# Tile 0's mixer in buffers of its own and the later mLSTM cells beside tile 0's experts, in a one-core hybrid block kernel

## Chip, cores and metric

The kernel runs on one core of a Trainium2 chip. The metric is the device time of one execution, in microseconds (us). Engines: PE (TensorE), DVE (VectorE), ACT (ScalarE), POOL (GpSimd) and SP (SyncE); the core has 16 DMA engines, fed by queues of SP, ACT and POOL.

## What is computed

One layer of a flow-matching backbone in float32, for 128 context tokens and 1024 latent tokens of width 1024:

```
h  = modulate(rmsnorm(x, n1), sh1, sc1)
mq, mk, mv, mo, gt, aq, ak, av = split_cols(h @ w_in)
m_out = mlstm_mixer(...)      # 4 heads of 128, forward and backward, h = h_f + h_b, rmsnorm, * sigmoid(mo)
a_out = attn_context(q, k, v, sink)                 # context tokens: one softmax over the 128 context keys + sink
a_out = attn_latent(rope(q), rope(k), v, kc, vc, sink)   # latent: 128 cached keys + neighbours within 128, + sink
x  = x + g1 * (concat(m_out, a_out) @ w_out)
h2 = modulate(rmsnorm(x, n2), sh2, sc2)
q  = (h2 @ w_q).reshape(N, 8, 256)                  # 8 heads, two halves of 128
sa, sb = q_a . sub_a, q_b . sub_b                   # 128 keys each; top 16 of each, then top 16 of the 256 sums
x  = x + g2 * sum over 8*16 experts of gate * gelu(h2 . u[e]) * v[e]      # rows u[e], v[e] of 1024 each
```

The context tokens use the conditioning row of c_ctx, the latent tokens that of c. The final mLSTM state of the context and its keys and values are outputs too. Each token picks its own 128 experts of 16384, so for one token 128 rows of u and 128 rows of v are fetched, 1 MB in all; for the 1152 tokens this is 1208 MB.

## The kernel before

**Stages.** The tokens are nine tiles of 128; tile 0 is the context, tiles 1 to 8 are latent. The stage `conditioning` computes the modulation rows, `project_in` (line 236) the input projection of all tiles, which it leaves in DRAM scratch (`qkT_scratch`, `kv_scratch`, `aqT_scratch`) at about 421 us. The stage `mix_and_experts` (line 654) does the rest and is the one that is changed.

**Generators.** Every engine runs the same five generators, each of which issues that engine's part of a step, and `drive` (line 715) calls them in one fixed order, so the order of every engine's queue is set in the source:

- `mixer(t)`: 15 sub-steps (SUBS). For each of 8 heads a score matmul over four key blocks of 128, mask and running minimum on DVE (L1560), exp on ACT, four transposes, four value matmuls; beside that the two mLSTM directions' h are loaded (L956 to L958), added and squared on POOL, normalised, multiplied by the sigmoid (L1095); then eight transposes, the w_out matmuls (L1241), and `at_x <- at_x, at_xn` (L1610), which is x1. Tile 0 goes through the same code with a mask of its own.
- `route(t)`: h2, the queries (16 chunks of w_q, 512 KB each), scores and the choice of experts. It has 34 steps (PART) for a first half of the heads' choice and 17 more for the second. The top-16 search begins with MAX8 (L1617) and ends, for each half of the experts, in `fx_eidx` (L1718) and `fx_gates` (L1729). For tiles 0 to 2 (STREAMED) w_q comes in chunks through two buffers `rt_wq` (four for the first eight chunks); from tile 3 on a resident copy is used, loaded from pair 30 (WQ_AT) of tile 2.
- `mlstm()`: 18 cells (here called units), forward and backward direction in turn, in three thirds each, and a finishing third of three steps; 57 thirds in all. A unit loads q, k, v (`ml_qkT`, `ml_k`, `ml_v`), and ends in `ml_h`, which ACT's queue stores (`h_scratch<-ml_h`). The first two units are tile 0; mixer 0 needs them alone, mixer t needs all units.
- `pair(t, r)`: 64 pairs per tile. A pair is two indirect gathers of 1 MB on POOL's queue (L1109, 128 rows of u and v each) into a ring of eight buffers, so that four pairs are under way; two dots on DVE (L1846), gelu (L1538) and the weights (L1542) on ACT, four accumulating matmuls on PE (L1396). The gather four pairs on is issued when PE has done the pair.
- `begin()`: what each engine waits for before the first gather.

**The order.** Six thirds of cells (LEAD), then the 15 sub-steps of mixer 0 with a third on each odd one; then the 34 first steps of route 0 with 43 thirds by `cells_beside`: one on each of the first six steps, 7 on the next eleven, 30 on the last seventeen. What is left of the cells comes next, then `begin`, whose POOL part waits for the h of all 18 units:

```
    pool.wait_ge(s_hd, UNITS)
    for d in range(2):
        pool.wait_ge(s_hst[d], 16 * TILES)
    for n in range(DEPTH):
        fetch(n)
```

After that the pairs run, and beside pair r of tile t `pace(t, r)` steps of the current tile's second choice and the next tile's route, and where `due(t, r)` says so one sub-step of the next mixer. In tile 0 mixer 1 stands beside pairs 0 to 14.

**Memory.** The mLSTM state buffers (`g.state`) and the mixer's (side "right", under an ExitStack `early`) take turns with others: the mixer has one set of buffers for all tiles, among it w_out (eight loads of 512 KB) and gate1, and w_q's resident copy overlaps it. The ring lies where the mLSTM state ends, so it can be filled only after the last cell. In PSUM the mixer's scores and tile 0's queries use `at_sP` (ST), the cells `fx_acc` and the two banks `rt_qP`.

## Time and profile before

| | us |
|---|---|
| median of 3 runs | 3687.01 |
| lowest and highest run | 3683.57, 3687.49 |
| the profiled execution, its own time | 3683.57 |
| its span | 3682.8 |
| stages before mix_and_experts, until about | 421 |
| first gather issued | 664.09 |
| first dot of experts | 673.56 |

The profile is one execution on the core. Its page gives the busy time of each engine: PE 72% of the span, DVE 67%, POOL 40%, ACT 27%. A second block shows the span in 40 slices of 92 us. A busy share of an engine says little here, since the program has two parts of different kind: until the first gather the engines work one after the other on small pieces with DMA used at 20 to 60%, afterwards the 1208 MB of expert rows pass.

### The profile page before, as it was taken

How to read it: one execution, taken by the hardware profiler on the slowest of the kernel's cores; microseconds unless marked ns; L12 is line 12 of the kernel's file. 1: busy time of each engine (PE TensorE's matmuls, PEld its weight loads, DVE VectorE, ACT ScalarE, POOL GpSimd, SP SyncE). 2: the span in 40 equal slices, each digit the busy share in tenths (PEclk: the TensorE clock that was granted, in tenths of full speed). 3: DMA queues.
4: the chain of work that ended last, by engine and by line, in shares of the span. 5: the costliest groups of instructions: out<-in, count | busy, mean ns of one | idle time of the engine just before them, and what ended most of it. 6: DMA issues, size and time to landing. Idle time of an engine off the chain costs nothing.

```text
span 3682.8 us, 31091 instructions
## 1 busy us (share of the span) xinstructions
PE 2644.4 (72%) x9770; PEld 1042.0 (28%) x9770; DVE 2453.7 (67%) x5523; ACT 990.0 (27%) x2700; POOL 1459.0 (40%) x1300
## 2 busy tenths in 40 slices
PE   7999888687877878866566567557656755775655
PEld 3455567333333333312121112112111211221111
DVE  3666435776787678648857677685767768576655
ACT  1223333442433244422122122212212221221111
POOL 0110023443454455434444444444444444444443
PEclk9999889899989989889799789879977987987677
DMA  7222446899999999999999999999999999999999
GB/s 299 95 97 94 163 125 204 333 410 422 416 421 426 425 412 420 389 424 414 427 427 427 427 423 427 422 417 424 416 427 420 427 420 423 424 417 427 411 427 380
DMA packets 224537, 1365.12 MB, mean 371 GB/s; under 512 B 25194, under 2 KB 36074, under 8 KB 75890
## 3 DMA queue, kind: packets, MB, share of 16 engines
q0 software_dynamic: 165888, 1208.03, 78.4%
q1 hardware_dynamic: 50992, 134.74, 10.1%
q10 hardware_dynamic: 7492, 20.36, 1.4%
q8 instruction: 77, 1.26, 0.1%
q14 instruction: 88, 0.72, 0.0%
HBM read 1334.05 MB, written 28.99 MB: 370 GB/s over the span
## 4 chain that ended last, share of the span: by engine, by line
DMA 40%; PE 20%; DVE 15%; issue 4%; POOL 4%; ACT 4%; SPq 0%; ACTq 0%; POOLq 0%; DVEq 0%
DMA fx_ring<-arg_uv,fx_eidx 38%; PE fx_acc L1396 11%; DVE fx_ring L1846 8%; POOL fx_ring L1109 4%; PE at_sP L1241 3%; ACT fx_weighted_pick L1542 2%; PE at_aP L1203 1%; DMA rt_wq<-arg_w_q 1%; DVE rt_rest L1708 1%; DVE rt_ab L1710 1%; DVE rt_rest L1706 1%; DMA rt_w_q<-arg_w_q 1%; PE at_sP L1269 1%; ACT fx_gelu L1538 1%; PE at_sP L1187 1%
## 5 line engine op out<-in xcount | busy, mean ns | idle before, releaser
L1396 PE MATMUL fx_acc<-fx_ring,fx_weighted_pick 128*64 128x512 f32 x4608 | 1417.7, 747 | 929.8 <-ACT fx_weighted_pick L1542 908.3
L1109 POOL DMA_INDIRECT fx_ring<-arg_uv,fx_eidx x1152 | 1317.0, 1143 | 1634.7 <-PE fx_acc L1396 1444.5
L1846 DVE CUSTOM_DVE_ANT_0 fx_ring<-fx_ring,fx_h 128x1024 f32<-128x1024 f32 x1152 | 1411.8, 1237 | 774.0 <-DMA fx_ring<-arg_uv,fx_eidx 769.5
L1396 PEld LDWEIGHTS fx_acc<-fx_ring,fx_weighted_pick 128*64 128x64 f32 x4608 | 327.0, 158 | 1903.7 <-ACT fx_weighted_pick L1542 1368.4
L1538 ACT ACTIVATE fx_gelu<-fx_dot 128x2 f32<-128x2 f32 x576 | 117.1, 203 | 2116.2 <-DVE fx_dot L1846 2115.7
L424 PE MATMUL in_z<-w_in,in_hT 128*128 128x512 f32 (+1 forms) x864 | 352.4, 566 | 7.3 <-PEq L97 7.3
L1542 ACT ACTIVATE fx_weighted_pick<-fx_weighted_pick,fx_gelu 128x64 f32<-128x64 f32 x1152 | 338.0, 340 | 55.1 <-ACT fx_gelu L1538 2.2
L424 PEld LDWEIGHTS in_z<-w_in,in_hT 128*128 128x128 f32 x864 | 163.6, 192 | 177.3 <-issue 172.0
L1269 PE MATMUL rt_qP<-rt_w_q,rt_h2T 128*128 128x512 f32 x384 | 193.6, 629 | 9.4 <-DMA rt_w_q<-arg_w_q 9.4
L384 POOL COPY in_turned<-in_heads 128x320 f32<-128x320 f32 x9 | 9.1, 1010 | 320.1 <-DVE in_heads L579 320.1
L1241 PE MATMUL at_sP<-at_w_out,at_mixT 128*128 128x512 f32 x288 | 133.3, 606 | 0.9 <-DVE at_mixT L1601 0.9
L1269 PEld LDWEIGHTS rt_qP<-rt_w_q,rt_h2T 128*128 128x128 f32 x384 | 66.8, 193 | 137.3 <-issue 126.3
L1838 DVE TENSOR_TENSOR fx_weighted_pick<-fx_pick,fx_gates 128x512 f32<-128x512 f32 x144 | 99.2, 689 | 2.4 <-DVE fx_gates L1729 0.7
L1846 DVE DVE_READ_ACCUMULATOR2_ANT fx_dot<- 128x1 f32 x1152 | 94.6, 82 | 0.0
L1560 DVE CUSTOM_DVE_ANT_0 at_s<-at_sP,at_mask,at_sink_negated 128x512 f32<-128x512 f32 x72 | 53.0, 750 | 60.7 <-PE at_sP L1187 50.9
L1538 ACT ACT_TABLE_LOAD x64 | 82.1, 1283 | 10.9 <-POOL ml_h L1129 9.7
L1269 PE MATMUL rt_qP<-rt_wq,rt_h2T 128*128 128x512 f32 x128 | 65.1, 632 | 15.1 <-DMA rt_wq<-arg_w_q 15.1
L1241 PEld LDWEIGHTS at_sP<-at_w_out,at_mixT 128*128 128x128 f32 x288 | 52.8, 191 | 78.1 <-issue 77.9
L1143 POOL TENSOR_TENSOR ml_k<-ml_k,ml_cols 128x512 f32<-128x512 f32 x18 | 18.7, 1039 | 141.2 <-ACT ml_cols L1506 108.9
L631 DVE SCALAR_TENSOR_TENSOR in_ada_acc<-in_ada_w,silu,in_ada_acc 128x1024 f32<-128x1024 f32 x56 | 70.1, 1292 | 0.3
L1203 PE MATMUL at_aP<-att_v,at_pT 128*128 128x64 f32 x432 | 67.8, 299 | 0.0
L1187 PE MATMUL at_sP<-att_kT,at_qT 64*128 64x384 f32 x144 | 65.4, 537 | 0.0
(300 smaller groups left out, 2450.4 us busy)
## 6 DMA issues: line engine op xcount, KB each, us to landing
rt_wq<-arg_w_q SPq DMA_DIRECT2D x44, 512.0 KB, 7.8
fx_ring<-arg_uv,fx_eidx POOLq DMA_INDIRECT x1152, 12.7
in_ada_w<-arg_w_ada SPq DMA_DIRECT2D x32, 512.0 KB, 4.0
ml_qkT<-qkT_scratch SPq DMA_DIRECT2D x18, 512.0 KB, 4.2
ada_w<-arg_w_ada SPq DMA_DIRECT2D x8, 1024.0 KB, 13.8
w_in<-arg_w_in SPq DMA_DIRECT2D x16, 512.0 KB, 16.4
rt_w_q<-arg_w_q SPq DMA_DIRECT2D x16, 512.0 KB, 32.7
kv_scratch<-in_kv ACTq DMA_DIRECT2D x9, 768.0 KB, 3.3
```

Source lines behind the costliest of these rows:

```text
L424: mm = pe.matmul(zp[b % 3][:, 0:n], hT[par][:, k, :], g.w_in[:, k, c0:c0 + n], start=(k == 0), stop=(k == KD - 1))
L631: dve.scalar_tensor_tensor(ada_acc[cnd][:], ada_w[m % AW][:], g.silu[:, k, cnd:cnd + 1], ada_b[:] if k == 0 else ada_acc[cnd][:], ALU.mult ...
L1109: pool.indirect_dma_start(out=ring[j][:], out_offset=None, in_=io.uv, in_offset=bass.IndirectOffsetOnAxis(ap=eidx[t % 2][:, i:i + 1], axis=0),
L1187: pe.matmul(ST[h % 2][:, P:4 * P], lhs, g.akT[half, t * P:t * P + 3 * P], start=True, stop=True).then_inc(s_sc, 1)
L1203: mm = pe.matmul(aP[:, h * ADH:(h + 1) * ADH], pT[h % 2][:, j * P:(j + 1) * P], rhs, start=(j == 0), stop=(j == 3))
L1241: mm = pe.matmul(ST[half][:], mixT[:, j, :], w_out[:, j, half * 512:(half + 1) * 512], start=(j == 0), stop=(j == KD - 1))
L1269: mm = pe.matmul(banks[half][b][:], hq2T[:, k, :], w[:, b * 512:(b + 1) * 512], start=(k == 0), stop=(k == KD - 1))
L1396: mm = pe.matmul(acc[b][cg * TOKS:(cg + 1) * TOKS, :], wsel[:, i % (2 * FILL), :], ring[i % GROUP][:, D + b * 512:D + (b + 1) * 512], star ...
L1538: act.activation(gelu[:, sl], dot[:, sl], ACT.Gelu_apprx_tanh).then_inc(s_gelu, 1)
L1542: last = act.activation(wsel[:, i, :], wsel[:, i, :], ACT.Copy, scale=gelu[:, i:i + 1])
L1838: dve.tensor_tensor(wsel[:, lo:lo + FILL, :], pick[:].unsqueeze(1).to_broadcast([P, FILL, TOKS]), gates[t % 2][:, r * NC:r * NC + FILL].un ...
L1846: dve.tensor_tensor_reduce(out=ring[j][:, 0:D], in0=ring[j][:, 0:D], in1=h2r[t % 2][cg][:], scale=1.0, scalar=0.0, op0=ALU.mult, op1=ALU.a ...
```

## The change

What it does, in five parts:

1. Tile 0's mixer has buffers of its own (`first`), all later tiles another set (`later`). w_out and gate1 are loaded for each set, and w_out is scaled by the norm weights for each. The ring lies where tile 0's mixer buffers end, no longer where the mLSTM state ends.
2. Tile 0's attention is `context(k)`: one key block, no mask, all heads in a few instructions.
3. The first eight chunks of w_q have six buffers (two `rt_wq`, the two rows of h2 of tile 0, one of tile 1, `gate2`), the next eight four.
4. The cells: 16 thirds stand beside mixer 0, 13 beside route 0, three after `begin`, the other 25 beside the first pairs of tile 0, one on each of 17 pairs and two after. `begin` waits for x1 of tile 0 (`at_x1_stored`), not for the cells.
5. In tile 0 mixer 1 stands beside pairs 23 to 37 and mixer 2 begins on even pairs after; route 1 begins at pair 38 (pair 17 before) with one or two steps per pair and ends at pair 63 (50 before). In tile 1 four pairs in five carry a sub-step; in tile 2 the resident w_q is loaded from pair 40 (30 before) and route 3 ends at pair 61 (57 before).

The core of the diff:

```diff
-    LEAD = 6
...
-    WQ_AT = 30
+    WQ_AT = 40
...
+    ROOM = 17640
+    CELL_PAIRS = 23
 
...
     def due(t, r):
+        if t == 0:
+            return r >= CELL_PAIRS and (r < CELL_PAIRS + SUBS or r % 2 == 0)
         if t == STREAMED - 1:
             return r < WQ_AT
-        return t == 0 and r < SUBS or 17 <= r < 23 or r >= 51 or r % 2
+        return r % 5 != 4
 
     def pace(t, r):
+        if t == 0:
+            return int(r < 17) if r < CELL_PAIRS + SUBS else 1 + int(r % 3 == 0)
         if t == STREAMED - 1:
-            return int(r < 17 or r >= WQ_AT - 1) + int(r >= 48 and r % 2)
+            return int(r < 17) if r < WQ_AT - 1 else 1 + r % 2
         return 1
 
-    def ahead(m):
-        return 2 * WQ if m < HQ else WQ
-
-    def cells_beside(k):
+    def buffer_of(m):
+        if m < HQ:
+            return m % 6
+        if m < NSIDE:
+            return (4, 5, 0, 1)[m % 4]
+        return m % WQ
+
+    def before(m):
+        return max((i for i in range(m) if buffer_of(i) == buffer_of(m)), default=None)
+
+    def loads(m):
+        return sum(buffer_of(i) == buffer_of(m) for i in range(m + 1))
+
+    def heads_before(t, context):
+        return context + (t - 1) * AH
+
+    def cells_in_mixer(k):
+        if k < 4:
+            return 3 if k == 0 else 2
+        return int(k < 10 or k == SUBS - 1)
+
+    def cells_in_route(k):
         if k < TURN:
             return 1
-        if k < TURN + 11:
-            return int(k % 3 > 0)
-        return 1 + int(k % 4 > 0)
+        return int(k % 4 == 0)
+
+    def cells_in_pair(r):
+        return 1 if r < 17 else 2
 
     def drive(begin, pair, mixer, route, mlstm):
 
         cells = mlstm()
-        for _ in range(LEAD):
-            next(cells)
         subs = chain.from_iterable(mixer(t) for t in range(TILES))
         for k in range(SUBS):
-            if k % 2:
+            for _ in range(cells_in_mixer(k)):
                 next(cells)
             next(subs)
         steps = chain.from_iterable(route(t) for t in range(TILES))
         for k in range(PART):
-            for _ in range(cells_beside(k)):
+            for _ in range(cells_in_route(k)):
                 next(cells, None)
             next(steps)
-        for _ in cells:
-            pass
         begin()
+        for _ in range(3):
+            next(cells)
         for t in range(TILES):
             left = steps_of(t) if t + 1 < TILES else steps_of(t) - PART
             for r in range(PAIRS):
                 for _ in range(min(pace(t, r), left)):
                     next(steps)
                     left -= 1
+                if t == 0 and r < CELL_PAIRS:
+                    for _ in range(cells_in_pair(r)):
+                        next(cells, None)
+                if t == 0 and r == CELL_PAIRS - 1:
+                    for _ in cells:
+                        pass
                 if due(t, r):
                     next(subs, None)
...
+        def mixer_buffers(n):
+            with ExitStack() as room:
+                def esb(name, shape, dt=F32):
+                    return room.enter_context(nc.sbuf_tensor(f"{name}_{n}", shape, dt))
+
+                m = Names()
+                m.w_out = esb("at_w_out", [P, KD, D])
+                m.aq = esb("at_qT", [P, AH // 2, P])
+                if n:
+                    m.mask = esb("at_mask", [P, 4 * P])
...
+        later = mixer_buffers(1)
+        with ExitStack() as room:
+            w_q = room.enter_context(nc.sbuf_tensor("rt_w_q", [P, KD, 2 * D], F32))
+        held = sb("mixer_room", [P, ROOM])
+        first = mixer_buffers(0)
         ring = [sb(f"fx_ring{i}", [P, 2 * D]) for i in range(GROUP)]
         gate2 = sb("fx_gate2", [P, D])
+        wq = [sb(f"rt_wq{i}", [P, HALF]) for i in range(WQ)]
         h2r = [[sb(f"fx_h2_0_{i}", [P, D]) for i in range(NC)], h2r1]
+        wq += h2r[0] + [h2r1[1], gate2]
...
-        w_q = sb("rt_w_q", [P, KD, 2 * D], side="right")
...
-        eP = acc[0][:].rearrange("p (h n) -> p h n", n=P)
-        oE = acc[0][:].rearrange("p (h n) -> p h n", n=256)
-        R = [x[:].rearrange("p (h n) -> p h n", n=256) for x in (acc[1], qP[0], qP[1])]
+        eP = other[0][:].rearrange("p (h n) -> p h n", n=P)
+        oE = other[0][:].rearrange("p (h n) -> p h n", n=256)
+        R = [x[:].rearrange("p (h n) -> p h n", n=256) for x in (other[1], qP[0], qP[1])]
         misc = cP[:].rearrange("p h n -> p (h n)")
-        qP0, cP0 = ST, aP[:].rearrange("p (h n) -> p h n", n=P)
+        first.ST, later.ST = acc, other
+        qP0, cP0 = acc, aP[:].rearrange("p (h n) -> p h n", n=P)
...
+                def load_weights(cnd):
+                    m = later if cnd else first
+                    sp.dma_start(m.gate1[:], g.gate_dram[cnd:cnd + 1, :].to_broadcast([P, D])).then_inc(s_g1, 16)
+                    for k in range(KD):
+                        sp.dma_start(m.w_out[:, k, :], io.w_out[k * P:(k + 1) * P, :]).then_inc(s_wo, 16)
...
+                        if k == 0 and t == 1:
+                            load_head(1)
+                            load_weights(1)
...
                 def begin():
-                    for d in range(2):
-                        sp.wait_ge(s_hst[d], 16 * TILES)
+                    sp.wait_ge(s_x1o, 16)
+                    sp.wait_ge(s_qd, NSIDE)
                     sp.dma_start(gate2[:], g.gate_dram[COND:COND + 1, :].to_broadcast([P, D])).then_inc(s_g2, 16)
...
                 def begin():
-                    pool.wait_ge(s_hd, UNITS)
-                    for d in range(2):
-                        pool.wait_ge(s_hst[d], 16 * TILES)
+                    pool.wait_ge(s_x1o, 16)
                     for n in range(DEPTH):
                         fetch(n)
...
                 def begin():
-                    pe.wait_ge(s_hd, UNITS)
+                    pe.wait_ge(s_qT, NG)
+                    pe.wait_ge(s_h2d, NC)
...
                 def begin():
-                    for d in range(2):
-                        dve.wait_ge(s_hst[d], 16 * TILES)
+                    pass
...
+                    def context(k):
+                        for b in range(2):
+                            for j in range(AH // 2):
+                                h = b * (AH // 2) + j
+                                half = slice(b * ADH, (b + 1) * ADH)
+                                cols_j = slice(j * P, (j + 1) * P)
+                                if k == 0:
+                                    mm = pe.matmul(m.ST[b][:, cols_j], m.aq[half, j, :], g.akT[half, P:2 * P],
+                                                   start=True, stop=True)
+                                    if j == AH // 2 - 1:
+                                        mm.then_inc(s_sc, 1)
+                                if k == 2:
+                                    if j == 0:
+                                        pe.wait_ge(s_p, (b + 1) * (AH // 2))
+                                    mm = pe.transpose(m.ST[b][:, cols_j], m.s[b][:, cols_j], g.ident[:])
+                                    if j == AH // 2 - 1:
+                                        mm.then_inc(s_pTp, 1)
+                                if k == 4:
+                                    if h == 0:
+                                        pe.wait_ge(s_pT, 2)
+                                    mm = pe.matmul(aP[:, h * ADH:(h + 1) * ADH], m.pT[b][:, cols_j],
+                                                   g.av[:, 1, b * ADH:(b + 1) * ADH], start=True, stop=True)
+                                    if h == AH - 1:
+                                        mm.then_inc(s_pv, 1)
+
...
+                        if t == 0 and k == 1:
+                            for h in range(AH):
+                                cols_h = slice(h % 4 * P, (h % 4 + 1) * P)
+                                if h == 0:
+                                    act.wait_ge(s_nm, 1)
+                                act.activation(m.s[h // 4][:, cols_h], m.ST[h // 4][:, cols_h], ACT.Exp, bias=m.nmx[:, h:h + 1],
+                                               scale=float(ADH) ** -0.5, accum_out=m.rs[:, h:h + 1]).then_inc(s_p, 1)
+                            act.wait_ge(s_dif, 1)
+                            act.activation(m.es[:], m.es[:], ACT.Exp).then_inc(s_es, 1)
...
+                        if t == 0 and k == 1:
+                            for b in range(2):
+                                dve.wait_ge(s_sc, b + 1)
+                                ca.link(dve.tensor_reduce(m.mx[:, 4 * b:4 * b + 4], m.ST[b][:].rearrange("p (h n) -> p h n", n=P),
+                                                          AX.X, ALU.max))
+                            ca.link(dve.tensor_scalar(m.mx[:], m.mx[:], -float(ADH) ** -0.5, None, ALU.mult))
+                            dve.tensor_tensor(m.nmx[:], m.mx[:], nsink[:], ALU.min).then_inc(s_nm, 1)
+                            dve.wait_ge(s_nm, 1)
+                            dve.tensor_tensor(m.es[:], sink[:], m.nmx[:], ALU.add).then_inc(s_dif, 1)
```

**What stands in the queues.** DVE at the end of tile 0's first choice of experts. Before (names with ml_ are cells, `fx_eidx` and `fx_gates` are what the gathers and their weights need, L1846 is the first dot):

```order
L1706 TENSOR_TENSOR rt_rest<-rt_pos_partf,rt_iota 128x1024
L1708 TENSOR_TENSOR rt_rest<-rt_rest,rt_val 128x1024 [waits rt_dve_chain]
L1710 TENSOR_REDUCE rt_ab<-rt_rest 128x64 [waits rt_dve_chain]
L1770 SCALAR_TENSOR_TENSOR ml_c<-ml_c,ml_tile_decay,rt_qP 128x129 [waits ml_c_done,ml_cols_ready,rt_dve_chain]
L1770 SCALAR_TENSOR_TENSOR ml_c<-ml_c,ml_tile_decay,rt_qP 128x129
L1775 TENSOR_TENSOR ml_num<-ml_num,fx_acc 128x258 [waits ml_intra_done,ml_inter_scaled]
...
L1718 SCALAR_TENSOR_TENSOR fx_eidx<-rt_ab 64x32 x4
...
L1729 TENSOR_TENSOR fx_gates<-rt_gexp,rt_gsum 64x32 x3
L1838 TENSOR_TENSOR fx_weighted_pick<-fx_pick,fx_gates 128x512 [waits fx_h2_rows_act,ml_h_stored1,fx_h2_rows_dve,ml_h_stored0,rt_route_done]
L1846 ISA fx_ring,fx_dot<-fx_ring,fx_h_0_0 128x1024 [waits fx_fetched0]
```

and now:

```order
L1813 TENSOR_REDUCE rt_ab<-rt_rest 128x64 [waits rt_dve_chain]
L1821 SCALAR_TENSOR_TENSOR fx_eidx<-rt_ab 64x32 [waits rt_dve_chain]
...
L1832 TENSOR_TENSOR fx_gates<-rt_gexp,rt_gsum 64x32 x3
L1857 TENSOR_TENSOR ml_e<-at_sP,ml_e 128x512 [waits ml_e_masked,ml_qk_done,rt_route_done]
L1873 SCALAR_TENSOR_TENSOR ml_c<-ml_c,ml_tile_decay,rt_qP 128x129 [waits ml_c_done,ml_cols_ready]
...
L1940 TENSOR_TENSOR fx_weighted_pick<-fx_pick,fx_gates 128x512 [waits fx_h2_rows_dve,fx_h2_rows_act]
L1948 ISA fx_ring,fx_dot<-fx_ring,fx_h_0_0 128x1024 [waits fx_fetched0]
```

The cell rows have left the way to `fx_gates`, the waits for stored h are gone, and one unit stands between the gates and the first dot.

POOL around the first gather, before:

```order
L1129 TENSOR_TENSOR ml_h<-ml_num,ml_den 128x512 [waits ml_den_ready,ml_h_stored0]
L1129 TENSOR_TENSOR ml_h<-ml_num,ml_den 128x512 [waits ml_den_ready,ml_h_stored1]
L1109 DMA fx_ring<-arg_uv,fx_eidx 128x2048 [waits ml_h_stored1,rt_route_done,ml_h_stored0,ml_h_ready]
L1109 DMA fx_ring<-arg_uv,fx_eidx 128x2048 x7
L1109 DMA fx_ring<-arg_uv,fx_eidx 128x2048 [waits fx_pair_done]
```

and now:

```order
L1162 DMA fx_ring<-arg_uv,fx_eidx 128x2048 [waits rt_route_done,at_x1_stored]
L1162 DMA fx_ring<-arg_uv,fx_eidx 128x2048 x7
L1196 TENSOR_TENSOR ml_k<-ml_k,ml_cols 128x512 [waits ml_load0,ml_cols_ready]
L1202 AFFINE_SELECT ml_e<-ml_e 128x512 [waits ml_e_ready]
L1175 COPY ml_rfix<-gate_rows 128x128 [waits ml_colT_done]
L1182 TENSOR_TENSOR ml_h<-ml_num,ml_den 128x512 [waits ml_den_ready,ml_h_stored1]
L1162 DMA fx_ring<-arg_uv,fx_eidx 128x2048 [waits fx_pair_done]
```

The first eight gathers wait for tile 0's choice and x1, and POOL's work of a unit stands among the later gathers.

DVE where tile 1's first gates are made, before (between the dots of pairs 50 and 51 of tile 0):

```order
L1846 ISA fx_ring,fx_dot<-fx_ring,fx_h_0_1 128x1024 [waits fx_fetched5]
L1846 ISA fx_dot 128x1
L1718 SCALAR_TENSOR_TENSOR fx_eidx<-rt_ab 64x32 x4
L1722 TENSOR_REDUCE rt_gsum<-rt_gexp 128x4 [waits rt_gate_exp,rt_dve_chain]
...
L1846 ISA fx_ring,fx_dot<-fx_ring,fx_h_0_0 128x1024 [waits fx_fetched6,rt_route_done]
```

and now:

```order
L1948 ISA fx_ring,fx_dot<-fx_ring,fx_h_0_1 128x1024 [waits fx_fetched7]
L1948 ISA fx_dot 128x1
L1821 SCALAR_TENSOR_TENSOR fx_eidx<-rt_ab 64x32 x4
...
L1832 TENSOR_TENSOR fx_gates<-rt_gexp,rt_gsum 64x32 x3
L1940 TENSOR_TENSOR fx_weighted_pick<-fx_pick,fx_gates 128x512 [waits fx_h2_rows_dve,fx_pair_done,fx_h2_rows_act,rt_route_done]
L1948 ISA fx_ring,fx_dot<-fx_ring,fx_h_1_0 128x1024 [waits fx_fetched0]
```

`fx_eidx` of tile 1 now stands behind the last dot of tile 0 (pair 63), and the gather of pair 0 of tile 1 waits for it (`rt_route_done`).

## Rows read from the trace of the kernel before

**Rows 1.** The page: span, DMA share in 40 slices (tenths), GB/s.
```profile
span 3682.8 us, 31091 instructions
...
DMA  7222446899999999999999999999999999999999
GB/s 299 95 97 94 163 125 204 333 410 422 416 421 426 425 412 420 389 424 414 427 427 427 427 423 427 422 417 424 416 427 420 427 420 423 424 417 427 411 427 380
```

**Rows 2.** The chain that ended last, by engine.
```profile
DMA 40%; PE 20%; DVE 15%; issue 4%; POOL 4%; ACT 4%; SPq 0%; ACTq 0%; POOLq 0%; DVEq 0%
```

**Rows 3.** The DMA view of 665 to 3683 us; last column us to landing.
```profile
DMA packets 183683, 1265.25 MB, mean 419 GB/s; under 512 B 20400, under 2 KB 20400, under 8 KB 36094
...
rt_wq<-arg_w_q SPq DMA_DIRECT2D x30, 512.0 KB, 8.1
```

**Rows 4.** SP's timeline: time, duration, line, out<-in.
```profile
472.32 0.33 SPq L956 DMA_DIRECT2D at_mix<-h_scratch  x1
```

**Rows 5.** DVE's timeline: start us, duration us; in brackets idle before and its releaser.
```profile
519.90 0.69 DVE L1610 TENSOR_TENSOR at_x<-at_x,at_xn 128x512 f32<-128x512 f32 x1
...
577.63 0.65 DVE L1617 MAX8 rt_val<-rt_scores 128x8 f32<-128x128 f32 x3
...
581.51 0.69 DVE L1754 TENSOR_TENSOR ml_e<-fx_acc,ml_e 128x512 f32<-128x512 f32 x1 [3.04 <-PE fx_acc L1366]
...
653.09 0.69 DVE L1754 TENSOR_TENSOR ml_e<-fx_acc,ml_e 128x512 f32<-128x512 f32 x1
...
659.78 1.52 DVE L1718 SCALAR_TENSOR_TENSOR fx_eidx<-rt_ab 64x32 uint32<-64x32 f32 x4
...
661.80 0.79 DVE L1729 TENSOR_TENSOR fx_gates<-rt_gexp,rt_gsum 64x32 f32<-64x32 f32 x4
...
673.56 1.23 DVE L1846 CUSTOM_DVE_ANT_0 fx_ring<-fx_ring,fx_h 128x1024 f32<-128x1024 f32 x1 [9.60 <-DMA fx_ring<-arg_uv,fx_eidx]
```

**Rows 6.** A window: us, busy PE, PEld, DVE, ACT, POOL; PEclk, DMA share, GB/s.
```profile
577.60:662.60 85.00, 68.64 (x480) 55.34 (x479) 60.23 (x211) 27.95 (x99) 26.99 (x35) 0.97 0.54 178
```

**Rows 7.** DVE's groups in 577.6 to 662.6 us.
```profile
L1770 DVE SCALAR_TENSOR_TENSOR ml_c<-ml_c,ml_tile_decay,rt_qP 128x129 f32<-128x129 f32 x36 | 10.9, 344 | 4.7 <-PE rt_qP L1375 4.5
...
L1775 DVE TENSOR_TENSOR ml_num<-ml_num,fx_acc 128x258 f32<-128x258 f32 x18 | 7.5, 417 | 0.0
...
L1754 DVE TENSOR_TENSOR ml_e<-fx_acc,ml_e 128x512 f32<-128x512 f32 x9 | 6.2, 689 | 18.6 <-PE fx_acc L1366 14.6 <-issue 3.9
...
L1779 DVE SCALAR_TENSOR_TENSOR ml_den<-ml_num 128x4 f32<-128x4 f32 x9 | 3.8, 422 | 0.3
```

**Rows 8.** POOL's timeline: the first gather.
```profile
664.09 1.14 POOL L1109 DMA_INDIRECT fx_ring<-arg_uv,fx_eidx  x1 [3.05 <-DMA h_scratch<-ml_h]
```

**Rows 9.** DMA issues of the whole span: count, KB each, us to landing.
```profile
ml_qkT<-qkT_scratch SPq DMA_DIRECT2D x18, 512.0 KB, 4.2
...
ml_k<-kv_scratch SPq DMA_DIRECT2D x18, 256.0 KB, 4.8
...
h_scratch<-ml_h ACTq DMA_DIRECT2D x18, 256.0 KB, 2.0
...
at_w_out<-arg_w_out SPq DMA_DIRECT2D x8, 512.0 KB, 9.5
...
at_qT<-aqT_scratch SPq DMA_DIRECT2D x9, 256.0 KB, 7.7
...
at_gate<-gate_scratch SPq DMA_DIRECT2D x2, 512.0 KB, 6.8
```

**Rows 10.** The page's groups: the dots beside the gathers, ACT's table loads.
```profile
L1846 DVE CUSTOM_DVE_ANT_0 fx_ring<-fx_ring,fx_h 128x1024 f32<-128x1024 f32 x1152 | 1411.8, 1237 | 774.0 <-DMA fx_ring<-arg_uv,fx_eidx 769.5
...
L1538 ACT ACT_TABLE_LOAD x64 | 82.1, 1283 | 10.9 <-POOL ml_h L1129 9.7
```

**Rows 11.** POOL, line 1095, in 421 to 664 us.
```profile
L1095 POOL TENSOR_TENSOR at_mix<-at_mix,at_sigmoid 128x512 f32<-128x512 f32 x1 | 1.3, 1274 | 0.1
```

**Rows 12.** POOL, line 1095, in 800 to 1500 us.
```profile
L1095 POOL TENSOR_TENSOR at_mix<-at_mix,at_sigmoid 128x512 f32<-128x512 f32 x6 | 12.8, 2140 | 0.5
```

367 lines of the change are left out of this document (188 added, 179 removed).

## The prediction

> **What bounds the kernel now.** I read the page first, for the two halves of the span. Until slice 8 the DMA engines are busy two to six tenths of the time; from there to the end every slice says 9, and where nothing disturbs them they move 427 GB/s [rows 1]. The DMA view of the stretch after the first gather gives 1265.25 MB in 3018 us, 419 GB/s on average [rows 3]. That half is bound by bytes: an engine's work there costs nothing unless it keeps the queue of gathers from being refilled, and every MB put there costs 1/427 GB/s = 2.34 us. The chain of waits agrees: DMA holds 40% of the span in it [rows 2]; the PE, DVE and ACT steps on it lie mostly between a landed gather and the issue of the one four pairs later, and so beside the others' transfers.
>
> The half before is bound by short dependent steps. In the last 85 us before tile 0's gates PE is busy 68.6, DVE 60.2, DMA 0.54 of the time [rows 6]: no engine is full, and the order decides. So the time is the moment of the first gather plus the bytes behind it, plus what bubbles there are. I take these terms in turn. The profiled execution's own time (3683.57) is 0.8 over its span and 3.4 under the median 3687.01.
>
> **Term 1, the first gather comes earlier.** It is issued at 664.09 [rows 8]. Three stretches lead there. (a) Until x1 of tile 0, at 520.6 [rows 5]. h of tile 0 is asked for at 472.32 [rows 4]; it waits for units 0 and 1 being stored, and that stays. Behind it stand eight heads over four key blocks with mask, now eight matmuls over one block, and 7 cell thirds instead of which 16 now lie partly before and partly inside the wait for h. I take 12 us off; the bounds are 0 (the h chain alone decides) and 20. (b) From x1 to the first MAX8 at 577.63, 57 us [rows 5]. 13 thirds stood beside these steps, now 9. One third costs 2.98 us: ml_e is at 581.51 and after eight more units at 653.09, 8.95 us a unit [rows 5]. Four thirds are 12; I take 10. (c) From there to the gates at 661.80, 85 us, in which nine units' worth of DVE work stands [rows 7]: 30 thirds by 2.98 are 89, so the cells set this stretch. Now four thirds stand there. DVE's own work for the choice is 60.2 less 10.9, 7.5, 6.2 and 3.8, about 32 [rows 6, 7], 36 with the small den rows not shown; with the four thirds and PE's scores I take 40, so 45 us go. (d) The gather waited 3.05 us for the last stored h, 1.5 of them behind the gates [rows 8]; that goes. Sum: 12 + 10 + 45 + 1.5 = 68, bounds 50 and 80. The first gather should be at about **596**.
>
> **Term 2, bytes moved behind the first gather.** From [rows 9]: w_out a second time 8 x 0.524 = 4.19 MB, gate1 0.52; tile 1's at_qT and mask, which stood in the first half, 0.52; the cells whose loads come after the gate, seven by 0.524 + 0.262 + 0.262 = 7.34 MB; ten h stores by 0.262 = 2.62. Together 15.2 MB, by 2.34 us **+36**. The second half has no free DMA time that could hide it.
>
> **Term 3, cells beside the first 21 pairs.** A pair's rows take 2.10 MB / 427 = 4.9 us; with the cells' bytes (one third per pair, 1.3 MB per three) some 6.0. Beside that DVE has two dots of 1.24 [rows 10], reads, fill, up to 2.1 of route steps and a third's 0.9, in all 5.4 to 5.7. ACT has to change its table between gelu and the cells' exp, 1.283 us each time [rows 10], perhaps twice a unit. All lie just under 6.0, so DMA should stay first; for the pairs where a third delays PE's four matmuls, and with them the next gather by more than the four pairs' slack, I put **+5**, bounds 0 and 31 (below).
>
> **Term 4, route 1 in pairs 38 to 63.** 34 steps in 26 pairs instead of one per pair, with w_q's chunks through two buffers that take 8.1 us to land [rows 3]. Two steps then need two chunks in a pair of 5 us every third pair; the mean need is 16 chunks in 22 pairs, 110 us, against 8.1 x 8 = 65 with two under way. **+2**, bounds 0 and 10.
>
> **Term 5, the boundary of tiles 0 and 1.** `fx_eidx` of tile 1 now stands behind the dots of pair 63. The gathers of tile 1 can only be asked for after it, so nothing is in flight when the last pair of tile 0 has landed. The dots are 1.2 more, from the start of the eidx rows to the end of the gates 2.8 (659.78 to 662.59 [rows 5]), and from the first issue to the first dot the trace shows 673.56 - 664.09 = 9.5 [rows 5, 8], of which 2.5 is the transfer itself: 1.2 + 2.8 + 7.0 = **+11**. Below, 5: some of the gates' work is done before the last row lands; above, 20, if route 1's last chunks are late too. The Trainium skill, page "DMA: Bandwidth & Descriptors", section "🔬 Anatomy of one DMA — SWDGE (gpsimd) path", gives a fixed cost of about 2.0 us per such DMA beside its bytes; by that the bubble would be some 6, an estimate from the page, and the sum 5 lower. The trace here, with 9.5 us for a first gather, speaks for more.
>
> **Term 6.** Route 3 ends at pair 61 of tile 2 instead of 57, still ahead of the last: **+1**, bounds 0 and 5. Later load of the resident w_q and the other places of mixer 1 and 2 cost nothing while DMA is full: the bytes are the same. The six buffers for w_q's chunks take waits away where PE is what is waited for; they are inside term 1(b). The second scaling of w_out is four DVE rows in tile 0, under the transfers.
>
> Sum: -68 + 36 + 5 + 2 + 11 + 1 = -13: 3683.6 - 13 = 3670.6 for the execution; on the median **3674**. 0.2%, about what a measurement of this kernel can tell from no change, is 7.4 us: the borders are 3679.6 and 3694.4.
>
> **The rivals.**
> *A, nothing comes back* (0.15). The gates stand in time, the cells hide: -68 + 36, about 3655. For it: DVE and ACT are each under a pair's time. Against: the order puts the eidx behind the last dot.
> *B, the cells set the pace of the first pairs* (0.16). ACT's part of a third waits for PE, which stands behind the same pair's matmuls, and ACT's gelu of the next pair stands behind that. If in two of three thirds this is served one after the other, 19 thirds by 2.98 are 57, less the 28 that their bytes already cost in term 2: +29, 3703, slower. It decides when pair and third together last longer than 6.1 us. For it: a third took 2.98 us even with no pair beside it, with DVE busy only 0.71 of that time [rows 6]. Against: four pairs lie in the ring.
> *C, mixer 0 ends no sooner* (0.09): h is asked for at the same time and the 16 thirds fill what the attention leaves. -68 becomes -56: 3686.
> *D, POOL slows DVE or is slowed* (0.10). POOL's multiply of mix and sigmoid took 1.27 us with DVE alone beside it [rows 11] and 2.14 beside the gathers and dots [rows 12], 0.87 more. Ten units have two such operations each: up to 17 us if they hold the next gather, 3691. By the Trainium skill, page "SBUF — State Buffer", section "🔬 SBUF: two separate sides", a DVE instruction with two SBUF inputs and a GpSimd one that reads SBUF share a port pair as an exclusive lock, and whichever starts first blocks the other for its whole length; the dots have two SBUF inputs, so by this rule each POOL row of a cell can wait a dot, or a dot a row. The two rows agree with it.
>
> **How the numbers follow.** The forecast has 0.50; its own range is 3658 to 3686, 0.38 of it faster, 0.12 within. A is faster (0.15). B is slower (0.16). C is 0.06 within, 0.03 slower. D is half within, half slower (0.05 each). So faster 0.53, same 0.23, slower 0.24. The range takes the low end of the forecast with half of A, 3648, and the high end of B's middle, 3706.
>
> **What would show it.** In the profile after: the first gather at about 596 (term 1), with x1 near 508, MAX8 near 555 and the gates near 595; about 1280 MB behind it (term 2); pairs of 6.0 to 6.2 us in the first 21 of tile 0 with DMA at 0.97 or more (term 3; B shows 7 or more with DMA at 0.8); a hole of about 11 us in DMA's use at the end of tile 0, with the first gather of tile 1 released by DVE (term 5). The prediction is wrong if the first gather is after 615, if the DMA share in the first pairs falls under 0.9, or if other such holes stand at later tiles.

## The result, and the profile after

The change takes 3729.61 us (median of 5 runs, 3723.91 to 3748.80) against 3687.01 (3683.57 to 3688.84): a ratio of 1.0124, 95% interval 1.0102 to 1.0147. It is slower by some 43 us; 3674 were forecast, 3648 to 3706 as the range. The profiled execution (span 3747.1) is the longest of the five, some 19 us above the median, so its losses below are somewhat larger than the usual ones.

The page of the change, the lines that answer to [rows 1] and [rows 2]:

```profile
span 3747.1 us, 30887 instructions
...
DMA  7222548999889999999999999999999999999998
GB/s 293 97 98 86 189 138 336 353 356 387 328 360 393 425 376 397 377 415 402 408 427 427 426 420 427 420 427 422 419 420 420 427 417 425 421 418 427 418 427 367
...
DMA 38%; PE 22%; DVE 15%; issue 5%; POOL 5%; ACT 4%; SPq 0%; ACTq 0%; POOLq 0%; DVEq 0%
```

The transfers begin sooner (336 GB/s in slice 7, 204 before), but slices 9 to 20, most of tiles 0 to 2, move 328 to 425 GB/s where they moved 389 to 427. From slice 21 on the two pages read alike.

The marks of tile 0 on DVE's and POOL's timelines of the change, which answer to [rows 5] and [rows 8] (start, duration):

```profile
502.46 1.29 DVE L1713 TENSOR_TENSOR at_x<-at_x,at_xn 128x512 f32<-128x512 f32 x1
...
548.20 0.68 DVE L1720 MAX8 rt_val<-rt_scores 128x8 f32<-128x128 f32 x3 [9.38 <-ACT rt_scores L1567]
...
587.55 0.79 DVE L1832 TENSOR_TENSOR fx_gates<-rt_gexp,rt_gsum 64x32 f32<-64x32 f32 x4
```

```profile
589.26 1.15 POOL L1162 DMA_INDIRECT fx_ring<-arg_uv,fx_eidx  x1 [11.52 <-DVE fx_gates L1832]
```

The first gather is issued at 589.26, 74.8 us sooner than before. The DMA view from 589 to 3747 us answers to [rows 3]:

```profile
DMA packets 192186, 1279.93 MB, mean 405 GB/s; under 512 B 21040, under 2 KB 24624, under 8 KB 44592
```

14.7 MB more lie behind the first gather, 34 us at 427 GB/s. To see where the rest went I cut both traces at the first gather of certain pairs: tile 0 at pairs 17, 26, 38 and 48, and tiles 1 and 2 whole. The columns are the stretch, its us, busy PE, PEld, DVE, ACT and POOL, granted clock, DMA share and GB/s. The change:

```profile
589.26:688.80 99.54, 66.67 (x331) 36.34 (x332) 77.13 (x220) 35.26 (x102) 51.07 (x55) 0.83 1.00 406
688.80:763.70 74.90, 48.54 (x202) 23.50 (x202) 46.48 (x95) 27.10 (x73) 29.73 (x31) 0.75 0.79 295
763.70:848.30 84.60, 59.83 (x235) 29.56 (x234) 39.72 (x74) 32.62 (x70) 32.05 (x29) 0.74 0.97 387
848.30:907.20 58.90, 44.51 (x162) 17.60 (x161) 33.51 (x63) 23.50 (x54) 25.52 (x21) 0.91 0.99 397
907.20:1047.20 140.00, 112.14 (x431) 50.22 (x429) 83.46 (x213) 38.71 (x94) 40.45 (x37) 0.84 0.79 312
1047.20:1415.60 368.40, 299.47 (x1204) 128.79 (x1203) 255.97 (x598) 139.58 (x328) 167.80 (x140) 0.89 1.00 401
1415.60:1802.20 386.60, 298.63 (x1200) 129.51 (x1198) 264.07 (x602) 138.72 (x331) 168.95 (x140) 0.88 0.98 397
```

The same pairs before (the last of tile 0, tile 1, tile 2):

```profile
936.30:1022.50 86.20, 67.79 (x287) 28.73 (x286) 62.20 (x119) 37.24 (x87) 46.33 (x37) 0.94 1.00 410
1022.50:1376.90 354.40, 282.35 (x1176) 121.84 (x1176) 262.15 (x599) 139.08 (x332) 175.91 (x141) 0.91 1.01 422
1376.90:1736.60 359.70, 273.45 (x1064) 110.05 (x1062) 251.57 (x580) 117.24 (x296) 165.41 (x136) 0.90 0.99 412
```

I call a stretch's length less what its bytes need at 427 GB/s its shortfall. For pairs 17 to 25 of the change it is 74.9 - 74.9 x 295/427 = 23.2 us; the rows of tile 0 give 4.9, 23.2, 7.9, 4.1 and 37.7, in all 78, where the kernel before has 10 in the same tile. Tile 1 has 22.4 (before 4.1), tile 2 27.2 (12.6). The excess is 68 + 18 + 15 = 101 us. The books close: -75 for the earlier start, +34 for the bytes and +101 for shortfalls is +60, the spans differ by 64.3, and most of the other 4 stand in tiles 3 to 8 (tile 3 alone has 3.1 us, 0.2 before). The forecast had 19 in the place of the 101. The DMA share hides a part of this: from 1329 to 1405 us, in tile 1 of the change, it is 0.98, as if nothing were amiss, and yet the rate is 365 GB/s, with 8.9 us (median) from a gather's issue to its landing. In the run e9 below the same pairs have 1.01, 425 GB/s and 12.8 us. So I go by the rate.

### The profile page after: what moved, and what is told of

The parts are those of the page before. It is cut to its first block, busy times and chain, and to the rows that moved or that the text cites. A ratio compares the mean times of both kernels' runs of the same rounds, so it can differ in the third digit from the quotient of the medians.

```text
span 3747.1 us, 30887 instructions
## 1 busy us (share of the span) xinstructions
PE 2677.5 (71%) x9682; PEld 1050.5 (28%) x9682; DVE 2453.9 (65%) x5516; ACT 1002.9 (27%) x2707; POOL 1449.4 (39%) x1300
## 4 chain that ended last, share of the span: by engine, by line
DMA 38%; PE 22%; DVE 15%; issue 5%; POOL 5%; ACT 4%; SPq 0%; ACTq 0%; POOLq 0%; DVEq 0%
DMA fx_ring<-arg_uv,fx_eidx 33%; PE fx_acc L1473 12%; DVE fx_ring L1948 8%; POOL fx_ring L1162 4%; PE at_sP L1318 3%; DMA rt_wq<-arg_w_q 2%; ACT fx_weighted_pick L1632 2%; PE rt_qP L1343 2%; PE at_aP L1255 1%; DVE rt_rest L1811 1%; DVE rt_ab L1813 1%; DVE rt_rest L1809 1%; DMA at_w_out<-arg_w_out 1%; DMA rt_w_q<-arg_w_q 1%; ACT fx_gelu L1628 1%
## 5 line engine op out<-in xcount | busy, mean ns | idle before, releaser
L1473 PE MATMUL fx_acc<-fx_ring,fx_weighted_pick 128*64 128x512 f32 x4608 | 1445.2, 760 | 894.9 <-ACT fx_weighted_pick L1632 867.2
L1343 PE MATMUL rt_qP<-rt_w_q,rt_h2T 128*128 128x512 f32 x384 | 194.7, 633 | 24.6 <-DMA rt_w_q<-arg_w_q 24.6
L1318 PE MATMUL at_sP<-at_w_out,at_mixT 128*128 128x512 f32 x256 | 122.5, 623 | 0.9 <-DVE at_mixT L1704 0.9
L1343 PE MATMUL rt_qP<-rt_wq,rt_h2T 128*128 128x512 f32 x128 | 77.6, 737 | 31.2 <-DMA rt_wq<-arg_w_q 29.3
L1628 ACT ACT_TABLE_LOAD x72 | 92.4, 1283 | 1.3
L1505 ACT ACTIVATE at_s<-at_s,at_negmax 128x512 f32<-128x512 f32 x64 | 45.9, 717 | 65.3 <-DVE at_negmax L1651 64.8
```

The lines of the kernel that those rows point to most:

```text
L1318: mm = pe.matmul(m.ST[half][:], m.mixT[:, j, :], m.w_out[:, j, half * 512:(half + 1) * 512], start=(j == 0), stop=(j == KD - 1))
L1343: mm = pe.matmul(banks[half][b][:], hq2T[:, k, :], w[:, b * 512:(b + 1) * 512], start=(k == 0), stop=(k == KD - 1))
L1473: mm = pe.matmul(acc[b][cg * TOKS:(cg + 1) * TOKS, :], wsel[:, i % (2 * FILL), :], ring[i % GROUP][:, D + b * 512:D + (b + 1) * 512], star ...
L1628: act.activation(gelu[:, sl], dot[:, sl], ACT.Gelu_apprx_tanh).then_inc(s_gelu, 1)
```

## The experiments

All kernels were run beside the kernel before on their own chip; ratios are to it. "e4" and so on are the labels. One percent is 37 us.

**e1, e2: what makes a pair with cells long.** In pairs 17 to 25 the change shows this (POOL's, DVE's and PE's timelines of one pair; `ml_e` is the cell's score matrix):

```profile
719.13 0.98 POOL L1162 DMA_INDIRECT fx_ring<-arg_uv,fx_eidx  x1 [4.99 <-PE fx_acc L1473]
720.42 0.93 POOL L1162 DMA_INDIRECT fx_ring<-arg_uv,fx_eidx  x1 [0.30 <-issue]
721.37 0.64 POOL L1202 TENSOR_SCALAR_AFFINE_SELECT ml_e<-ml_e 128x512 f32<-128x512 f32 x1
```

```profile
722.11 0.69 DVE L1857 TENSOR_TENSOR ml_e<-at_sP,ml_e 128x512 f32<-128x512 f32 x1 [9.93 <-POOL ml_e L1202]
722.72 1.61 DVE L1948 CUSTOM_DVE_ANT_0 fx_ring<-fx_ring,fx_h 128x1024 f32<-128x1024 f32 x1
```

```profile
715.17 3.68 PE L1473 MATMUL fx_acc<-fx_ring,fx_weighted_pick 128*64 128x512 f32 x8 [4.03 <-ACT fx_weighted_pick L1632]
...
720.19 1.06 PE L1442 MATMUL at_sP<-ml_qkT 128*128 128x128 f32 x8
```

DVE stands idle for 9.93 us ahead of its row `ml_e`, which needs two things. One is POOL's select: POOL needs 0.64 us for it, but it is queued behind the gathers, and these wait for PE's matmuls of the pair; it ends at 722.01. The other is PE's `at_sP<-ml_qkT`, queued behind the same matmuls of the pair; it ends at 721.25, so without POOL the row would have waited almost as long. DVE's next dots stand behind the waiting row, and PE's next matmuls behind the dots. So the pairs run one after the other, and four buffered pairs don't help. The clock has a part in it: the eight matmuls of the pair took 3.68 us here and 1.94 one pair before (from 707.86), and the granted clock of the stretch is 0.75 (0.87 before the change).

e1 puts POOL's part ahead of the pair's gather (`early` is true on POOL alone):

```diff
+                if early and t == 0 and r < CELL_PAIRS:
+                    for _ in range(cells_in_pair(r)):
+                        next(cells, None)
                 pair(t, r)
...
-                if t == 0 and r < CELL_PAIRS:
+                if not early and t == 0 and r < CELL_PAIRS:
```

> The changed kernel, with the cells' POOL part ahead of the pair's gather instead of behind it. The profile of the change shows 31 us in which the DMA engines had nothing to move in pairs 17 to 37 of tile 0 (23 of them in pairs 17 to 25, where two thirds stand beside a pair), and DVE waiting 9.9 us for POOL's ml_e, which stands behind a gather that waits for PE. Theory POOL (that queue order sets the pace): some 20 us less than the change, about 3709. Rival PE (DVE waits for PE's part of the third, which stands behind the pair's matmuls, and POOL's place does not matter): no change, 3730. Rival BYTES (only bytes): 3730.

Measured: 3711.64, ratio 1.0054 (1.0034 to 1.0074), 0.7% or 26 us under the change. Pairs 17 to 25 in its windows:

```profile
691.90:754.40 62.50, 43.58 (x196) 22.06 (x197) 41.76 (x84) 22.08 (x61) 33.34 (x30) 0.81 0.89 349
```

Their shortfall is 11.4 instead of 23.2. POOL's queue order is shown as a cause, though not the only one: POOL's select now ends at 715.3, and the same row of the cell waits all the same, for PE:

```profile
720.30 0.69 DVE L1860 TENSOR_TENSOR ml_e<-at_sP,ml_e 128x512 f32<-128x512 f32 x1 [7.79 <-PE at_sP L1445]
```

What rival PE of the expectation named is thus seen in what is left. The 26 us are not all this wait's either: between the two profiles the shortfall falls by 17 us in pairs 17 to 37, but also by 6 in pairs 56 to 63 and by 8 in tile 2, where both kernels have the same order. Those 14 stay unexplained.

e2 moves DVE's part one pair back instead (`drive(..., late=1)` on DVE: the thirds of pair r - 1 behind pair r).

> The changed kernel, with DVE's part of each third one pair later than the other engines' part. Theory POOL and rival PE both expect a gain, since DVE's dots of the next pair no longer stand behind rows that wait for POOL or PE: 15 to 25 us less than the change, 3705 to 3715, pairs 17 to 25 at 6 us instead of 8.3. Rival BYTES: none, 3730. If e1 gives nothing and this gives 20, it is PE; if both give it, POOL's queue.

Measured: 3733.86, ratio 1.0129 (1.0104 to 1.0153): no gain. The profiled run, the shortest of its four (3723), has a shortfall of 13.5 in pairs 17 to 25, but the median does not follow. The row behind another pair's dots was no cure; both theories expected one, so this miss stays unexplained in its detail.

**e3: no pair with two thirds.** Eight more thirds ahead of the first gather, and CELL_PAIRS = 17, so that mixer 1 and route 1 come six pairs sooner.

```diff
-    CELL_PAIRS = 23
+    CELL_PAIRS = 17
-        return int(k % 4 == 0)
+        return int(k % 4 == 0) + int(k > 17 and k % 4 > 1)
```

> The changed kernel with eight more thirds of cells ahead of the first gather, so that none of tile 0's pairs carries two, mixer 1 starts at pair 17 instead of 23 and route 1 at pair 32 instead of 38 (it ends near pair 57). Theory PACING (the loss comes from pairs that carry more than a pair's time holds): first gather 10 to 24 us later, but the bubbles of pairs 17 to 25 (23 us), 48 to 55 (13) and 56 to 63 (25) mostly gone: 3690 to 3700. Rival BYTES: 15 us slower than the change, 3745.

Measured: 3722.66, ratio 1.0091 (1.0072 to 1.0111), 12 us better than the change by the ratios, whose intervals just overlap. PACING had 3690 to 3700 and missed. First gather at 612.8, 23.5 later; the hole at the end of tile 0 goes (1.0 in pairs 56 to 63), but 13 us remain in pairs 48 to 55, as many as in the change, and pairs 0 to 16 have 11 (4.9 in the change, also with one third each; 0.3 in e5 below, with neither cells nor sub-steps). A third as such isn't free, even one per pair.

**e4: the layout with the old order.** All cells ahead of the first gather, and `due`, `pace` and WQ_AT as before:

```diff
-        begin()
-        for _ in range(3):
-            next(cells)
+        for _ in cells:
+            pass
+        begin()
-    WQ_AT = 40
+    WQ_AT = 30
```

> The changed kernel's buffers, context attention, w_q buffers and gate, with all cells ahead of the first gather and the order of sub-steps and route steps of the kernel before (resident w_q from pair 30 of tile 2). Theory PACING: first gather at 640 to 652, tile 1's w_out and gate1 and masks (5.2 MB, 12 us) in the second half, no bubbles beyond the 10 us of the kernel before in tile 0: 3675 to 3690, faster than the change by 40 to 55 us. Rival BUFFERS (the new layout itself costs in the second half, through aliased buffers): 3710 or more, with bubbles at tiles 1 and 2.

Measured: 3677.55, ratio 0.9968 (0.9957 to 0.9980). It is faster than the kernel before, by 12 us, and 57 faster than the change. Its windows of tile 1 and its first gather:

```profile
1010.80:1365.10 354.30, 281.42 (x1177) 120.31 (x1176) 260.68 (x599) 139.26 (x333) 174.12 (x141) 0.91 1.01 422
```

```profile
643.95 1.14 POOL L1160 DMA_INDIRECT fx_ring<-arg_uv,fx_eidx  x1 [9.14 <-DVE fx_gates L1830]
```

422 GB/s as before: the new buffers cost nothing there, and rival BUFFERS falls. All of the change's loss comes from its order.

**e5: which part of the order.** e4 with the change's tables.

> The changed kernel with all cells ahead of the first gather (as in e4), but with the change's own tables for sub-steps, route steps and the resident w_q. It splits e4's gain of 52 us over the change. First gather at 644 as in e4. Theory PACING says two things are lost by the change: bubbles beside cells (about 30 us in pairs 17 to 37) and bubbles of compressed route 1 and of denser sub-steps in tiles 1 and 2 (about 65 us); only the first is gone here, and it is paid with 55 us of later start less 26 us of bytes: 3725 to 3735. Rival CELLS (the thirds beside the pairs are the whole loss): 3680.

Measured: 3720.76, ratio 1.0085 (1.0064 to 1.0106). The tables alone cost 1.0085 - 0.9968, 43 us; the cells beside the pairs, with their earlier start, another 14 (1.0124 - 1.0085; these two intervals just overlap). PACING (3725 to 3735) came near and CELLS (3680) was wrong: the larger part isn't with the cells at all. The first 17 pairs, which carry neither cells nor sub-steps here, run at 426 GB/s.

**e6, e10, e14: the late route 1.** e6 ends it three pairs sooner (`1 + int(r % 2 == 0)`).

> The changed kernel with route 1 in tile 0 at one step more on every second pair from 38 instead of every third, so that it ends at pair 60 and not 63. Theory BOUNDARY (the hole is the eidx behind the last dot, 11 us): 8 to 11 us less than the change, 3720. Theory DENSITY (ACT's gelu stands behind rows that wait for PE's queries, 13.7 us of them at pair 61): the hole moves ahead and stays, 3725 to 3740.

Measured: 3729.67, ratio 1.0101 (1.0079 to 1.0123); against the change's 1.0124 the intervals overlap. In its profile the shortfall of pairs 56 to 63 falls from 24.6 to 11.3, and that of pairs 48 to 55 grows from 13.1 to 20.1. The hole moves ahead and most of it stays, as DENSITY said.

e10 takes only the late and compressed route 1 into e4, e14 a late one that is not compressed (34 steps in pairs 30 to 63):

```diff
 # e10, pace(0, r)
+        if t == 0 and r >= 17:
+            return 0 if r < 38 else 1 + int(r % 3 == 0)
 # e14
+        return int(t > 0 or r < 17 or r >= 30)
```

> e4 with route 1 begun at pair 38 and compressed as in the change, ending at pair 63; everything else as e4. Theory DENSITY: bubbles of 27 to 35 us in pairs 38 to 63 as in the change and e5, nearly all of the tables' cost in tile 0, 3705 to 3712. Rival BOUNDARY (only the eidx behind the last dot): 11 us, 3689.

> e4 with route 1 at one step per pair from pair 30, so that it ends at pair 63 without compression. By the prediction's term 5 (eidx behind the last dot): 11 us more than e4, 3686 to 3691, a DMA hole of that size ahead of tile 1's first gather and none before pair 60. If the hole of the change comes from compression alone: 3677 to 3680.

Measured: e10 3700.13, ratio 1.0030 (1.0015 to 1.0045), 23 us over e4; e14 3680.31, 0.9980 (0.9970 to 0.9989), 4 over e4. Pairs 48 to 63 of e10, and of e14:

```profile
913.20:1047.60 134.40, 111.60 (x475) 52.89 (x474) 84.32 (x218) 43.49 (x102) 41.87 (x36) 0.93 0.86 336
```

```profile
913.80:1027.90 114.10, 101.19 (x463) 48.52 (x461) 88.26 (x229) 46.66 (x108) 41.71 (x37) 0.93 0.94 390
```

Shortfalls of 29 and 10 us (e4: 4). DENSITY had 3705 to 3712 for e10 and BOUNDARY 3689: the measured 3700 lies between. The boundary alone costs a few us (the intervals of e14 and e4 overlap), the compression some 19. In the change's trace the rows of PE, ACT and POOL show how:

```profile
1009.74 5.68 PE L1343 MATMUL rt_qP<-rt_wq,rt_h2T 128*128 128x512 f32 x8 [2.51 <-DMA rt_wq<-arg_w_q]
...
1021.09 3.78 PE L1343 MATMUL rt_qP<-rt_wq,rt_h2T 128*128 128x512 f32 x4 [3.80 <-DMA rt_wq<-arg_w_q]
```

```profile
1024.90 1.09 ACT L1555 ACTIVATE rt_scores<-rt_qP 128x512 f32<-128x512 f32 x2 [13.74 <-PE rt_qP L1343]
1025.88 0.20 ACT L1628 ACTIVATE fx_gelu<-fx_dot 128x2 f32<-128x2 f32 x1
```

```profile
1031.51 0.94 POOL L1162 DMA_INDIRECT fx_ring<-arg_uv,fx_eidx  x1 [11.76 <-PE fx_acc L1473]
...
1047.15 0.94 POOL L1162 DMA_INDIRECT fx_ring<-arg_uv,fx_eidx  x1 [13.47 <-DVE fx_gates L1832]
```

ACT waits 13.74 us for PE's queries, and the gelu of a pair whose dots ended at 1023 stands behind it; PE's matmuls of that pair and POOL's refill follow. PE in its turn waits for the chunks of w_q: in pairs 48 to 63 it was idle for them 18.5 us (five times) in the change, 10.4 (four times) in e10, and in e14 only its weight loads waited, 2.5 us. So two things come with the compression, the place in the queues and late chunks, and these runs do not separate them.

**e9, e13, e17: tiles 1 and 2.** e9 is e4 with 52 sub-steps in tile 1 instead of 41 and 19 in tile 2 instead of 30; e13 is e4 with the late resident w_q and the change's pace beside it; e17 is e4 with all tables of tiles 1 and 2, that is 52 sub-steps in tile 1 and 40 in tile 2, which needs 28 in tile 0 (pairs 0 to 14 and 51 to 63).

```diff
 # e9, due
+        if t == 1:
+            return r % 5 != 4
 # e13
-    WQ_AT = 30
+    WQ_AT = 40
 # e17: both, in tile 2 r < WQ_AT (40 sub-steps), and in tile 0
+        return r < SUBS or r >= 51
```

> e4 with 52 sub-steps of the mixer beside tile 1's pairs instead of 41 (the density of the change), and 19 instead of 30 beside tile 2's. The prediction put such a shift at nothing. Theory DENSITY (a sub-step's PE and ACT rows stand ahead of a pair's matmuls, and two of three pairs already carry one with a route step): tile 1 has 10 to 18 us more of DMA bubbles, tile 2 some 3 to 5 less: 3684 to 3692 against e4's 3677.6. Rival FREE (no cost while DMA is full): 3677.

> e4 with the resident w_q loaded from pair 40 of tile 2 instead of 30 and route 3 at one or two steps per pair from 39, ending at 61, as in the change. In the change PE waited 24.6 us for the resident w_q in tile 2. If that is the missing part of the tables' cost: 3690 to 3697 against e4's 3677.6, with 10 to 20 us more of bubbles in tile 2. If DMA stays busy with the w_q chunks meanwhile: 3678 to 3682.

> e4 with the change's tables for tiles 1 and 2 together: 28 sub-steps in tile 0 (pairs 0 to 14 and 51 to 63), 52 in tile 1, 40 in tile 2, resident w_q from pair 40 with route 3 ending at 61. Theory INTERACTION (sub-steps up to pair 40 of tile 2, with the w_q load behind them): the missing 20 us are here, 3692 to 3700. Rival TILE 0 (they come only with the late route 1 and the sub-steps beside it): 3675 to 3682.

Measured: e9 3675.37, ratio 0.9963 (0.9950 to 0.9977), my DENSITY falls; e13 3677.13, 0.9976 (0.9964 to 0.9987), within 3 us of e4; e17 3704.32, 1.0033 (1.0017 to 1.0049), 24 us over e4. Tile 1 of e9 and of e17, which have the same `due` there:

```profile
1011.90:1367.10 355.20, 305.08 (x1308) 138.61 (x1307) 266.51 (x622) 157.10 (x360) 173.48 (x142) 0.93 1.01 422
```

```profile
996.90:1370.20 373.30, 313.62 (x1251) 134.25 (x1252) 266.88 (x612) 142.35 (x338) 165.33 (x141) 0.90 1.00 402
```

A shortfall of 4 against 22 us with as many sub-steps and the same pace. What differs in the source is the count with which tile 1 begins, 49 sub-steps in e9 and 28 in e17, so the same pairs carry other sub-steps. I looked for the loss where they meet the route's query steps. A pair of e17 (1271 to 1283 us) has a query of four matmuls that waited 4.5 us for its chunk and eight transposes ahead of the pair's own matmuls:

```profile
1275.61 3.78 PE L1343 MATMUL rt_qP<-rt_wq,rt_h2T 128*128 128x512 f32 x4 [4.52 <-DMA rt_wq<-arg_w_q]
1279.19 1.91 PE L1245 MATMUL at_sP<-ident,at_s 128*128 128x128 f32 x8
1281.03 2.05 PE L1473 MATMUL fx_acc<-fx_ring,fx_weighted_pick 128*64 128x512 f32 x8
```

But the four pairs after it lost only 2.5 us. 6 of the 22 us stand in pairs 16 to 23 and 11 in pairs 48 to 63, where hardly a query stands (none from 1087 to 1133 us, four matmuls from 1283 to 1359); tile 1 of the change loses its 22 in the same places. So the two runs show that the number of sub-steps alone is not the cause; the phase is what is left, and which meeting costs the time stays open. Nor is tile 1 all of e17: its tile 2 has a shortfall of 30 us, against 13 in e13 and 14 in e4. INTERACTION had named tile 2 alone, and no run has tile 2's 40 sub-steps by themselves.

**e7, e8, e11, e12: is there a better place for some of the cells?** e7: nine thirds beside pairs 0 to 8, POOL early, route 1 from pair 24. e8: e4 with the old count of w_q buffers (4, then 2). e11 and e12: the last one or two units of e4 behind the issue of the first gathers:

```diff
 # e11, e12
-        for _ in cells:
-            pass
         begin()
+        for _ in cells:
+            pass
```

> e4's layout with nine thirds beside pairs 0 to 8, one each, POOL's part ahead of the gather as in e1; mixer 1 in pairs 9 to 23, route 1 from pair 24 at one step per pair (ends at pair 57), the resident w_q from pair 30 of tile 2, eight sub-steps moved to tile 1. Theory PACING: first gather some 16 us ahead of e4's 644, 9 us of that paid in bytes, no new bubble: 3668 to 3676, faster than e4. Rival: any third beside the pairs costs more than it saves: 3680 to 3690.

> e4 with four buffers for the first eight chunks of w_q and two after, as in the kernel before, instead of six and four. If the six buffers carry part of e4's earlier gather: first gather 3 to 10 us later than 644, time 3681 to 3687. If the queries wait for PE and the cells alone: no change, 3677.

> e4 with the last unit and the finishing steps (6 of 57 thirds) behind the issue of the first gathers, in the 10 us in which DVE waits for the first rows. Theory: first gather 9 to 14 us earlier, 1.3 MB at most (3 us) more behind it, no bubble, since the ring fills for 20 us while the unit is done: 3668 to 3673. Rival (a unit ahead of the first dots delays the refill of the ring): 3677 to 3682.

> As e11 with the last two units and the finishing steps (9 thirds) there. They take 18 to 27 us, about what the ring holds (four pairs, 20 us). First gather 15 to 20 us earlier than e4's 644; if the ring covers them, 3664 to 3670; if POOL's part of the units, behind eight gathers of 1.25 us each, comes late, a bubble of 10 us or more and 3675 to 3680.

Measured: e7 3686.76, ratio 0.9992 (0.9982 to 1.0002); e8 3675.04, 0.9955 (0.9938 to 0.9971); e11 3677.94, 0.9970 (0.9956 to 0.9983); e12 3675.79, 0.9969 (0.9955 to 0.9983). The six buffers carry nothing: with four the first gather stands at 642.7, with six at 644.0. Moving units behind the gate brings the gather 10 (e11) and 16 us (e12) forward and gives it all back: their shortfalls of pairs 0 to 16 are 10.7 and 12.2 against 4.7, and the 2.3 and 3.6 MB more behind the gate cost 5 and 8 us. e7 has its first gather at 617.8, 26 us ahead of e4, and loses more than that: 9 us of bytes, 10 more of shortfall in tile 0 (most of it in pairs 17 to 25, behind the cells' pairs) and 14 more in tile 1, where no cell stands but eight more sub-steps. Its rival had the right number; that the thirds themselves cost it is not shown.

**e15, e16, e18: what is worth keeping.** e15 puts `context(k)` into the kernel before, and nothing else; e16 adds the 16 thirds beside mixer 0; e18 has 18.

```diff
 # e16, drive of the kernel before
-        for _ in range(LEAD):
-            next(cells)
-            if k % 2:
-                next(cells)
+            for _ in range(cells_in_mixer(k)):
+                next(cells)
```

> The kernel before with tile 0's attention over its one key block (the change's context(k)) and nothing else: one set of mixer buffers, ring on the mLSTM state, old tables, old w_q buffers. x1 of tile 0 some 15 us earlier than 520.6 and the first gather at 645 to 652; without the 5.2 MB (12 us) that e4 loads twice: 3668 to 3675, faster than the kernel before by 0.3 to 0.6% and at least as fast as e4. If the layout carries e4's gain: no change, 3687 to 3690.

> e15 with 16 thirds of cells beside mixer 0 as in the change, instead of 13. Three thirds fewer are left ahead of the first gather: 3 to 9 us off e15 if the attention leaves room for them (first gather 640 to 645, 3662 to 3670), no change if mixer 0 is delayed by as much.

> e16 with five thirds instead of three on mixer 0's first sub-step (18 in all). If the wait for h leaves room there, two thirds (6 us) fewer ahead of the gates: 3657 to 3661. If mixer 0 is delayed by as much: 3662 to 3665.

Measured: e15 3674.25, ratio 0.9964 (0.9951 to 0.9977); e16 3662.68, 0.9939 (0.9915 to 0.9963); e18 3669.79, 0.9941 (0.9922 to 0.9961). The first gathers of e15 and e16:

```profile
652.25 1.14 POOL L1112 DMA_INDIRECT fx_ring<-arg_uv,fx_eidx  x1 [3.04 <-DMA h_scratch<-ml_h]
```

```profile
643.16 1.15 POOL L1115 DMA_INDIRECT fx_ring<-arg_uv,fx_eidx  x1 [9.17 <-DVE fx_gates L1788]
```

x1 of tile 0 is ready at 508.1 and 505.1, the three thirds bring the gates another 8.6 us forward. e16 has the lowest ratio, 22 us under the kernel before. Its interval overlaps those of e8, e15 and e18, so the order among these is not shown. It starts with e4's first gather but moves 1263.61 MB behind it where e4 moves 1268.41, which is the second w_out and gate1: 4.8 MB are 11 us, the difference of their ratios (0.0029). e18 is no better: its first gather stands at 648.0, later than e16's, so there is no room for more.

## Why the prediction was wrong

The gain and the bytes were priced rightly. What failed are terms 3 to 6, the price of the work set beside the gathers: 19 us together, where the profiles show 101.

**Term 1** was right: 74.8 us were gained, 68 forecast. x1 at 503.8 (508), 44.4 us on to MAX8 (47) and 40.1 from there to the end of the gates (40).

**Term 2** was right: 14.7 MB of 15.2.

**Term 3 failed.** It priced a pair by adding up each engine's busy time, all under 6.0 us, and concluded that DMA stays first. The first 17 pairs, with one third each, bear it out (shortfall 4.9). In pairs 17 to 25 the shortfall is 23.2 and in 26 to 37 7.9, against 1.9 and 1.3: some 28 us instead of 5. I took the mean over 21 pairs and so did not look at the four that carry two thirds, and I followed the wait on ACT and left out POOL's queue, although the order rows of POOL ahead of the prediction show the cell rows behind the gathers. Rival B had the size (29; by its own working it should have been 34, since term 2 holds 23 us of the cells' bytes and not 28), but spread it over the first 21 pairs, where the loss stands in pairs 17 to 37. Its mechanism was right in its first link only: ACT's part of the cell did wait 4.83 us for PE (before 719.94), whose cell matmuls stand behind the pair's. The gelu waited for DVE's dots (4.44 us before the one at 725.52) and not for ACT's cell rows, and POOL's queue, whose order e1 shows to be worth 26 us in all, was not in it. What keeps 11 us in these pairs in e1 stays open. Rival D, the port, was not needed: POOL's select took 0.64 of the 9.93 us, and its two multiplies of a unit took 1.05 and 1.03 us (medians) beside the dots, 1.04 each before. What the Trainium skill says in "SBUF — State Buffer", section "🔬 SBUF: two separate sides", was not tested here by itself.

**Terms 4 and 5 failed by size and share.** Together they had 13; e10 shows 23. Their order was wrong as well: the boundary got 11 and cost 4 (e14), the compression got 2 and cost 19. Term 4 compared mean times of chunk loads with the time at hand; in the trace PE did wait for single chunks (18.5 us in pairs 48 to 63), and two heavy steps in one pair put its queries ahead of the pair's matmuls and ACT's copy of them ahead of its gelu. As to the boundary, the 9.5 us from issue to first dot of one case were taken as the rule (7.0 without the transfer); in the change that way is 1047.15 to 1053.12, 6.0 us. The rule of the Trainium skill, "DMA: Bandwidth & Descriptors", section "🔬 Anatomy of one DMA — SWDGE (gpsimd) path", by which the bubble would be some 6 (an estimate from its 2.0 us), came nearer than my 11 to the 4 us of e14.

**Term 6 failed, and with it a sentence.** "Later load of the resident w_q and the other places of mixer 1 and 2 cost nothing while DMA is full." For more sub-steps in tile 1 at e4's phase (e9) and for the late w_q (e13) that holds; taken together as the change has them they cost 24 us (e17), 18 us of its shortfall in tile 1 and 16 in tile 2 over e4's. DMA is full only as long as every pair's chain through four engines stays under the ring's four pairs; which steps break that here is not known.

So of the 57 us between e4 and the change, about 43 come from the tables (23 from route 1, 24 from tiles 1 and 2, measured apart), 14 from the cells beside the pairs net of their earlier start. The sum of the parts is near the whole, though each ratio is uncertain by 4 to 9 us either way.

## What to carry to other kernels

When a phase is bound by a ring of transfers that is refilled by consumers, price a step moved into it by the queues and not by busy time: for each engine, which row stands behind the moved row, and who waits for that; an engine that both issues the refills and does a part of the moved work is one place where a closed loop forms, and the engine whose work releases the refills is another. Look at the fullest pair, not at the mean. And split a change of several parts: here the shorter context attention and three earlier thirds were worth 22 us, and all else took 68 away.

## What the runs showed beyond that

The same code can run at different clocks, and it shows in the transfers. Pairs 52 to 63 of tile 1 in e15 and e16 are the same work:

```profile
1309.00:1382.10 73.10, 59.76 (x233) 28.12 (x234) 48.44 (x93) 35.41 (x77) 33.16 (x29) 0.77 0.95 380
```

```profile
1285.70:1353.30 67.60, 53.24 (x233) 24.89 (x234) 48.68 (x93) 35.24 (x77) 34.61 (x28) 0.85 1.00 408
```

At a mean granted clock of 0.77 PE is busy 6.5 us longer with as many matmuls and the stretch is 5.5 us longer; in e17 the eight matmuls of a pair took 3.68 us at one place and 1.94 at the next, about the ratio of the two levels, 1.2 and 2.4 GHz. Other runs with the same tables for tile 1 agree: these pairs have a shortfall of 3 us at a clock of 0.85 (the kernel before, e4, e16) and of 7 to 8 at 0.77 (e8, e10, e15). Whether the lower clock makes the pairs late, or late pairs the lower clock, no run here separates. e15's span is 3688.8, 14 us above its own median, and so its profile shows more shortfall than its time. That is why shortfalls of single profiles are used here for places, and the ratios for sizes. The other thing not expected: the first dot of tile 1 came 6.0 us after its gather's issue, the first of tile 0 9.5 before the change, and in the change 6.0 too (589.26 to 595.26).
